# Second attention block in split float32r: 21 weight tiles with low parts by GpSimd, and the gate table's zeros issued by GpSimd

## What is computed

```python
mod = silu(c) @ ada_w + ada_b              # six vectors: shift, scale, gate, twice
h = modulate(rmsnorm(x, norm1_g), shift1, scale1)
q, k, v, cb, cc, cu = split(h @ w_in)      # widths 512, 128, 128, 512, 512, 512
q, k = rope(rmsnorm(q per head)), rope(rmsnorm(k per head))
attn = sliding_window_attention(q, k, v, sinks)     # window 128, 8 query heads, 2 key heads
conv = cb * short_conv(cc * cu, conv_w)             # 3 taps
merged = concat(rmsnorm(attn), rmsnorm(conv))
x = x + gate1 * (merged @ w_out)
h2 = modulate(rmsnorm(x, norm2_g), shift2, scale2)
x = x + gate2 * peer(h2, ...)   # 16384 experts, 16 chosen by each of 8 heads
```

## Time and profile before

| What | Value |
|---|---|
| profiled execution, its span | 2427.28 us, 2425.5 us |
| TensorE busy, of the span | 2390.9 us (99%) |
| VectorE, ScalarE, GpSimd busy | 1435.7, 874.2, 1045.5 us |
| mean granted TensorE clock | 0.99 |
| feed-forward of the first block | 518.8 to 881.4 us |
| second block up to the output product | 888 to 1122 us |

### The profile page before, as it was taken

The page is one execution under the profiler, slowest core; times in us unless marked ns, Lnnn a source line. Parts: engine busy times, 40 slices in busy tenths (PEclk is TensorE's granted clock), DMA queues, the critical chain, the costliest instruction groups (busy, mean ns, idle before and its releaser), DMA issues.

```text
span 2425.5 us, 33627 instructions
## 1 busy us (share of the span) xinstructions
PE 2390.9 (99%) x11435; PEld 1464.0 (60%) x11435; DVE 1435.7 (59%) x2831; ACT 874.2 (36%) x1385; POOL 1045.5 (43%) x739
## 2 busy tenths in 40 slices
PE   8999899999999999999999999999999999999999
PEld 6888677658888875445454444444444466666665
DVE  4412455456867556544949894222222399999988
ACT  3222223232232242223135655544544433333332
POOL 0001111010000020000888888888888175578666
PEclk9999889999999999999999999999999999999999
DMA  7240100265656312942436666666666799999997
GB/s 207 70 72 1 53 10 10 70 178 156 191 176 205 87 53 70 345 174 87 87 48 153 154 148 153 155 147 154 155 147 156 257 401 375 370 361 375 374 361 287
DMA packets 437701, 426.49 MB, mean 176 GB/s; under 512 B 104809, under 2 KB 359913, under 8 KB 437489
## 3 DMA queue, kind: packets, MB, share of 16 engines
q1 hardware_dynamic: 353456, 332.85, 43.0%
q0 software_dynamic: 84160, 92.58, 15.5%
HBM read 364.28 MB, written 61.05 MB: 175 GB/s over the span
## 4 chain that ended last, share of the span: by engine, by line
PE 96%; DVE 2%; ACT 1%; SPq 0%; issue 0%; DMA 0%; POOL 0%; DVEq 0%; ACTq 0%; POOLq 0%
PE psum L1474 9%; PE psum L1475 9%; PE psum L1476 9%; PE psum L1499 7%; PE psum L1497 7%; PE psum L1498 7%; PE psum L1249 6%; PE psum L889 6%; PE psum L1206 5%; PE psum L1208 5%; PE psum L1207 5%; PE psum L1455 4%; PE psum L1106 1%; PE psum L1083 1%; PE psum L1062 1%; PE psum L1122 1%
## 5 line engine op out<-in xcount | busy, mean ns | idle before, releaser
L786 POOL DMA_INDIRECT dense_gates<-arena x384 | 607.2, 1581 | 151.6 <-issue 116.7
L1474 PE MATMUL psum<-arena 128*128 128x512 bf16 x1024 | 389.4, 380 | 0.0
L1476 PE MATMUL psum<-arena 128*128 128x512 bf16 x1024 | 387.1, 378 | 0.0
L1475 PE MATMUL psum<-arena 128*128 128x512 bf16 x1024 | 386.6, 378 | 0.0
L2545 DVE TENSOR_TENSOR arena<-arena,psum 128x1024 bf16<-128x1024 f32 x124 | 151.5, 1221 | 352.2 <-ACT psum L1855 351.7
L1498 PE MATMUL psum<-arena,low 128*128 128x384 bf16 x1024 | 333.8, 326 | 0.0
L1499 PE MATMUL psum<-arena,low 128*128 128x384 bf16 x1024 | 333.8, 326 | 0.0
L1497 PE MATMUL psum<-arena,low 128*128 128x384 bf16 x1024 | 333.8, 326 | 0.0
L1871 ACT ACTIVATE low<-low 128x1024 bf16<-128x1024 f32 x128 | 135.3, 1057 | 296.3 <-PE psum L1499 282.6
L814 POOL DMA_INDIRECT arena<-gelu_spill,arena x128 | 178.3, 1393 | 87.5 <-DMA gelu_spill<-cst 43.3
L806 POOL DMA_INDIRECT arena<-in_v,arena x128 | 166.3, 1300 | 103.0 <-DVE arena L2592 77.5
(11 more groups left out here) (377 smaller groups left out, 3937.0 us busy)
## 6 DMA issues: line engine op xcount, KB each, us to landing
arena<-in_uT SPq DMA_DIRECT2D x128, 512.0 KB, 4.6
low<-in_v SPq DMA_DIRECT2D x128, 512.0 KB, 5.3
gelu_spill<-cst SPq DMA_DIRECT2D x128, 256.0 KB, 3.4
arena<-in_ada_w POOLq DMA_DIRECT2D x12, 2048.0 KB, 9.3
dense_gates<-arena SPq DMA_DIRECT2D x4, 6144.0 KB, 40.1
arena<-gelu_spill SPq DMA_DIRECT2D x128, 192.0 KB, 5.2
arena<-dense_gates SPq DMA_DIRECT2D x128, 192.0 KB, 6.7
low<-in_w_in SPq DMA_DIRECT2D x20, 1024.0 KB, 7.4
```

Source lines behind the costliest of these rows:

```text
L786: pool.indirect_dma_start(gate_cells, bass.IndirectOffsetOnAxis(ap=cell_of[:, n:n + 1], axis=0), gate_of[:, n:n + 1], None, compute_op=ALU ...
L1474: mm(psum[:, bank, :], hi[:, c, :], h2hi[:, c, :], start=c == 0, stop=False)
L1475: mm(psum[:, bank, :], hi[:, c, :], h2lo[:, c, :], start=False, stop=False)
L1476: last = mm(psum[:, bank, :], lo[:, c, :], h2hi[:, c, :], start=False, stop=c == DC - 1)
```

## The change

Twenty-one tiles of the second block take the split form: query tiles 2 and 3, the key tile, all tiles of `cc`, `cu` and `cb`, and output tiles 2 to 7 (`ITEMS_2`, in TensorE's order). High parts are written by ScalarE (`split_high_2`; in the loop at the steps in `SPLIT_AT`), low parts by GpSimd (`split_low_2`), into the three buffers of the feed-forward. The activations get high parts from ScalarE (`bhi`) and low parts from VectorE (`blo`), once for the normed input and once for the merged one. The last norm leaves VectorE and becomes two multiplications over all of `xT2` on GpSimd, after its ninth low part. The weight fills wait for GpSimd's low parts (`fw_lo`), and the next fill is issued earlier than before in places. The zeros of `dense` are written by 16 transfers on GpSimd's queue, of 8 rows of experts each: two after each of the last four `load_ada`, and eight more after these. The buffers are laid out anew for it (those lines are left out here).

```diff
+        ITEMS_2 = [("q", 2), ("q", 3), ("k", 0)]
+        ITEMS_2 += [(what, j) for j in range(4) for what in ("cc", "cu")] + [("cb", j) for j in range(4)]
+        ITEMS_2 += [("o", f) for f in range(2, DC)]
+        SPLIT_AT = [(6, 7), (8,), (9, 10), (11,), (12, 13), (14,), (15, 16), (17,)]
...
@@ SyncE
+                sp.wait_ge(S["fw_lo"], F_ALL + 2 + k)
                 fill(F_CU2 + k, ...
-                     "p2_ready", 4 if k == 0 else 5 + SC)
-            fill(F_CB2, halves(F_CB2, w2[:, :, c_cb:c_cb + 512]), "p2_ready", 5 + SC + 2)
-            sp.wait_ge(S["pool_step"], 10)
-            for q in range(4):
-                sp.dma_start(io["dense"][q * 32:(q + 1) * 32, :, 0:DEN].rearrange("i j t -> j i t"),
-                             zeros.unsqueeze(1).to_broadcast([P, 32, DEN])).then_inc(S["zeroed"], 16)
+                     "p2_ready", 2 if k == 0 else 5 + SC)
+            fill(F_CB2, halves(F_CB2, w2[:, :, c_cb:c_cb + 512]), "fw_lo", F_ALL + place_2["cc", 2])
...
-                fill(F_OUT2 + k, ..., "p2_ready", 5 + SC + 4 * (k + 1))
+                fill(F_OUT2 + k, ..., "fw_lo", F_ALL + place_2[("cb", 0) if k == 0 else ("o", 2)])
...
@@ GpSimd
+            def clear(q):
+                pool.dma_start(io["dense"][q * 8:(q + 1) * 8, :, 0:DEN].rearrange("i j t -> j i t"),
+                               zeros.unsqueeze(1).to_broadcast([P, 8, DEN])).then_inc(S["zeroed"], 16)
...
                 load_ada(k)
+                if k == 6:
+                    pool.wait_ge(S["tab"], 1)
+                    step(pool.memset(zeros, 0.0))
+                elif k > 7:
+                    pool.wait_ge(S["pool_step"], 10)
+                    clear(2 * k - 16)
+                    clear(2 * k - 15)
+            for q in range(8, 16):
+                clear(q)
...
+            def split_low_2(i):
+                pool.wait_ge(S["fw_hi"], F_ALL + i + 1)
+                pool.tensor_tensor(fwl[i % SPLITS], raw_2(i)[1], fwh[i % SPLITS], ALU.subtract).then_inc(S["fw_lo"], 1)
+
+            for i in range(place_2["o", 5]):
+                split_low_2(i)
+                if i == 8:
+                    pool.wait_ge(S["x2_ready"], 1)
+                    pool.tensor_tensor(xT2, xT2, col_ln[:, 0:DC].unsqueeze(2).to_broadcast([P, DC, SEC]), ALU.mult
+                                       ).then_inc(S["x2_ready"], 1)
+                    pool.wait_ge(S["x2_ready"], 2)
+                    pool.tensor_tensor(xT2, xT2, r2[:, 1, :].unsqueeze(1).to_broadcast([P, DC, SEC]), ALU.mult
+                                       ).then_inc(S["x2_ready"], 1)
+                elif i == 16:
+                    add_square(sqc, 1, "m_sq", 2)
             for c in range(1, DC - 1):
                 add_square([u2[:, i, :] for i in range(DC)], c, "sq_ready", 3 * DC + c + 1)
+                if 2 <= c < 5:
+                    split_low_2(place_2["o", c + 3])
...
@@ TensorE (product becomes product_2 for the 21 tiles)
+            def product_2(bank, i, sig, between=None):
+                pe.wait_ge(S["fw_lo"], F_ALL + i + 1)
+                wh, wl = fwh[i % SPLITS], fwl[i % SPLITS]
                 for c in range(DC):
                     if between and c == 4:
                         between()
+                    mm(psum[:, bank, :], wh[:, c, :], bhi[:, c, :], start=c == 0, stop=False)
+                    mm(psum[:, bank, :], wh[:, c, :], blo[:, c, :], start=False, stop=False)
+                    last = mm(psum[:, bank, :], wl[:, c, :], bhi[:, c, :], start=False, stop=c == DC - 1)
+                last.then_inc(S[sig], 1)
...
@@ ScalarE
+            def split_high_2(i):
+                if i < SPLITS:
+                    act.wait_ge(S["ffn_ps"], F_ALL)
+                else:
+                    sig, count = done_2(i - SPLITS)      # product i - 3 has ended
+                    act.wait_ge(S[sig], count)
+                n, w = raw_2(i)
+                if i == 0 or raw_2(i - 1)[0] != n:
+                    act.wait_ge(*fill_done(n))
+                f_(fwh[i % SPLITS], w, ACT.Copy).then_inc(S["fw_hi"], 1)
+            for c in range(DC):
+                act.wait_ge(S["shifted"], c + 1)
+                f_(bhi[:, c, :], u2[:, c, :], ACT.Copy).then_inc(S["h2_hi"], 1)
+                if c >= DC - SPLITS:
+                    split_high_2(c - (DC - SPLITS))
...
                 ins.then_inc(S["a_tc"], 1)
+                for i in SPLIT_AT[s]:
+                    split_high_2(i)
...
+            for c in (4, 5, 6, 7, 0, 1, 2, 3):
+                act.wait_ge(S["m_done"], (c + 4) % DC + 1)
+                f_(bhi[:, c, :], mix[:, c, :], ACT.Copy).then_inc(S["h2_hi"], 1)
...
@@ VectorE
             modulated(0, col_n1, DC)
+            for c in range(DC):
+                dve.wait_ge(S["h2_hi"], c + 1)
+                dve.tensor_tensor(blo[:, c, :], u2[:, c, :], bhi[:, c, :], ALU.subtract).then_inc(S["h2_split"], 1)
             dve.wait_ge(S["std_ready"], 5)
             settle(dve.reciprocal(r2[:, 1, :], r2[:, 1, :]))
-                if j < 4:
-                    last_norm(2 * j)
-                    last_norm(2 * j + 1)
...
+            dve.wait_ge(S["zeroed"], 256)                # ahead of the attention loop
...
+            for k, c in enumerate((4, 5, 6, 7, 0, 1, 2, 3)):
+                dve.wait_ge(S["h2_hi"], DC + k + 1)
+                dve.tensor_tensor(blo[:, c, :], mix[:, c, :], bhi[:, c, :], ALU.subtract).then_inc(S["h2_split"], 1)
             for f in range(DC):
                 dve.wait_ge(S["out2_done"], f + 1)
+                dve.wait_ge(S["x2_ready"], 3)
```

More of the change, by code:

```diff
@@ L135, in program @@
         with nc.sbuf_tensor("split", [P, SPLIT_FLOATS], F32R) as split:
+            pass
+        with nc.sbuf_tensor("below", [P, BELOW_2], F32), nc.sbuf_tensor("split_2", [P, 2 * DC * SEC], F32R) as split_2:
             pass
@@ L271, in program @@
         keep = top[0]
+        sq2 = carve(2, SEC)
+        tm2 = carve(2, SEC)
+        pT2 = carve(2, PER * P)
+        assert top[0] == CUT + BELOW_2
+        bhi, blo = (split_2[:, k * DC * SEC:(k + 1) * DC * SEC].rearrange("p (c t) -> p c t", c=DC) for k in range(2))
+        top[0] += 2 * DC * SEC
+        mxs, nms, rss, ess = (carve(PER) for _ in range(4))
+        assert top[0] <= ffn_end - 2 * SPLITS * DC * P
+        top[0] = ffn_end
+        cosT, sinT, angT = (carve(SEC) for _ in range(3))
+        assert top[0] <= over_rstd - MOD_W
+        vt2 = angT.rearrange("p (a b) -> p a b", a=SC)
+        ex = carve(PER, 2 * P)
+        mix = carve(DC, SEC)
+        y2 = carve(CW // P, SEC)
+        over_zeros = arena_floats - (DC * SEC + P + SEC + DEN)
+        assert top[0] <= over_zeros
+        top[0] = over_zeros + DEN
         qkr = carve(5, SEC)
-        vt2 = carve(SC, P)
         prod = carve(2, SEC + CK2 - 1)
         cc = carve(2, SEC)
[L276 to L285, removed]
         top[0] = over_rstd + 2 * TP
         kf, posi = carve(SEC), carve(SEC)
+        zeros = kf[:, 0:DEN]
         assert top[0] <= base2
@@ L316, in program @@
         gate_of = carve(SEC)
-        zeros = carve(DEN)
+        assert top[0] == over_zeros, (top[0], over_zeros)
+        top[0] += DEN
         slot_row = carve(P).bitcast(U32)
@@ L393, in raw_done, with raw_2, done_2 @@
             return S[f"landed{r}"], before + 32 * (e // RAWS + 1)
+        F_ALL = len(ITEMS_F)
+        ITEMS_2 = [("q", 2), ("q", 3), ("k", 0)]
+        ITEMS_2 += [(what, j) for j in range(4) for what in ("cc", "cu")] + [("cb", j) for j in range(4)]
+        ITEMS_2 += [("o", f) for f in range(2, DC)]
+        place_2 = {item: i for i, item in enumerate(ITEMS_2)}
+        def raw_2(i):
+            what, j = ITEMS_2[i]
+            n = {"q": F_Q2, "k": F_KV2, "cc": F_CU2 + j // 2, "cu": F_CU2 + j // 2, "cb": F_CB2, "o": F_OUT2 + j // 4}[what]
+            if what in ("cc", "cu"):
+                w = slot[n % 2].rearrange("p (g c n) -> p g c n", g=2, c=DC)[:, what == "cu"]
+                return n, w[:, :, j % 2 * P:(j % 2 + 1) * P]
+            return n, slot_cols(n, 256 if what == "k" else 512)[:, :, j % 4 * P:(j % 4 + 1) * P]
+        def done_2(i):
+            what, j = ITEMS_2[i]
+            return {"q": ("p2_ready", j + 1), "k": ("p2_ready", 5), "cc": ("ffn_ps", F_ALL + j + 1),
+                    "cu": ("p2_ready", 5 + SC + j + 1), "cb": ("p2_ready", 5 + SC + 4 + j + 1), "o": ("out2_done", j + 1)}[what]
         def chunks_of(i):
@@ L1278, in _ @@
             for f in range(2, 5):
-                n, k = (F_Q2, f) if f < 4 else (F_KV2, 0)
-                if k == 0:
-                    pe.wait_ge(*fill_done(n))
+                if f == 2:
+                    pe.wait_ge(S["h2_split"], DC)
                 pe.wait_ge(S["p2_taken"], f - 1)
-                product(f % 2, slot_cols(n, 512 if f < 4 else 256), slice(k * P, (k + 1) * P), u2, "p2_ready")
+                product_2(f % 2, f - 2, "p2_ready")
                 qk_mean(f - 1)
```

55 lines of the change are left out of this document (22 added, 33 removed).

## The result

| | us |
|---|---|
| before, median of 20 runs | 2427.17 (2418.12 to 2428.89) |
| changed, median of 20 runs | 2434.5 (2426.21 to 2438.15) |
| ratio, 95% interval | 1.0027 (1.0017 to 1.0037) |
| profiled execution, its span | 2434.32, 2432.5 |

The changed kernel is slower by 0.27%, where 3.5 us faster was forecast. Its trace is cut at the same landmarks as that of before: the first and last start of one line's instructions, as in the earlier trace rows.

What follows compares the result with a forecast made beforehand. TensorE was taken to bound the kernel, holding 96% of the chain of waits. Terms -2.6 + 1.3 - 7.2 + 3 + 2 = -3.5 on 2427.28 gave 2423.8 us profiled, 2423.2 as median; range 2405 to 2435.

Steps and rivals of the forecast that it cites:

- Feed-forward and DMA: Zeros on GpSimd's queue between the modulation loads of the feed-forward: last load up to 7 us late, priced at +2 us.
- The rival of the slow modulation load: Feed-forward's second part: below about 205 GB/s VectorE's wait for the last modulation load decides; 2430 to 2438 us, chance 0.12.
- a TensorE gap in the feed-forward over 5 us: One of the signs listed beforehand that would show the forecast wrong.
- Stage A: From the first norm to the first scores, 4 tiles: -5.6 us before waits, -2.6 with them.
- Stage B: The eight attention steps, 11 tiles: 17.7 us gained against 19.0 of waits, so +1.3 us.
- the clock: TensorE's granted clock falls to 0.50 after a long wait in the attention loop: +3 us, bounds 0 and 6.
- The exclusion: VectorE operations with two SBUF inputs and GpSimd tensor operations exclude each other; attention steps wait 19.0 us in all.
- Step 2: Attention step with GpSimd's two 4096-column multiplications, 7.4 us each; they hold up VectorE's small operations and TensorE waits 9.1 us.
- steps 1, 3, 5 and 7: Attention steps where GpSimd's subtractions hold up VectorE's small operations: waits of 2.9, 1.8, 2.1 and 3.1 us.
- Stage C: Merge and output, 6 tiles: -8.4 us before waits, -7.2 with them.
- The zeros leave SyncE's queue at no gain: Taking the zeros off SyncE's queue gains nothing, since nothing on the chain of waits waits for them.
- The forecast's rule of two SBUF inputs: VectorE operations with two SBUF inputs and GpSimd tensor operations exclude each other for their whole length.

Runs made afterwards that it cites:

- x2: The kernel before with only the zeros moved, to 16 GpSimd transfers in the feed-forward; 2442.13 us, ratio 1.0066 to before.
- x1: The changed kernel with the zeros again written by four SyncE transfers in the second block, the 21 tiles kept; 2419.2 us, ratio 0.9971 to before.
- x3: The changed kernel with the same 16 clears spread, four behind one modulation load, then one per later feed-forward tile; 2420.87 us, ratio 0.9969 to before.

## Why the prediction was wrong

**The step that failed is "Feed-forward and DMA", a term of +2 that measured +14.1.** It asked who waits for the zeros and who stands behind them in GpSimd's queue, and found the modulation load, 0 to 4 us late, and nobody else: "Clears 6 to 15 (15.7 MB, 70 us at 225) pass by about 865, ahead of VectorE's new wait at the loop". It named the transfers and their 70 us, and didn't ask which other queue uses the same DMA engines in those 70 us. The feed-forward's weight loads do, one pair for every two tiles, and their landing is what TensorE's splits wait for. The rival of the slow modulation load reached the right total (2430 to 2438) by the wrong road: the slowest load landed after 13.6 us, and its sentence "weight loads share the engines" had the sharing the wrong way round. It was set aside with "every load of before lands at 225 GB/s beside them"; 9.3 us, from which that figure comes, is the median, and the slowest of before's twelve took 13.7. The sign of error that the prediction named, "a TensorE gap in the feed-forward over 5 us", is what the trace shows (7.98 the longest).

The waits are not the whole of it: they sum to 10.8. Behind the longest the granted clock is 0.50, and twelve products start 0.43 us apart instead of 0.23, which is 2.5 us of the other 3.3.

**Stage A, forecast -2.6, measured -3.9.** The last two low parts of the activations meet GpSimd as worked out (L2424 twice in 4.49 us), and the second tile starts at 918.6, where the forecast, moved by the 13.2 us of the later feed-forward, gave 919.5.

**Stage B, forecast +1.3 and +3 for the clock, measured +4.0 with both in it.** The exclusion was right, but the sum is right by luck, from terms that were each off. Step 2 waits 9.61 (9.1 forecast); steps 1, 3, 5 and 7 wait 1.77, 0, 1.22 and 1.92 (2.9, 1.8, 2.1 and 3.1): 14.5 in all instead of 19.0. The tiles took back some 3 us of that. The forecast set 7.10, a recorded length, against 5.49, a distance between starts. By distances a tile of the loop took 6.97 us (1018.03 to 1025.00, before) and takes 5.62 (1022.87 to 1028.49, after), so eleven gain 14.9, not 17.7; the forecast's own "29.4 us at most" for all 21 was less than the 31.7 that its three stages add up to. The clock, 8 us at 0.50, cost 4 us, more than the +3. Together -14.9 + 14.5 + 4 is 3.6 of the 4.0. The multiplications took 7.02 and 8.91 (7.4 each), the low part 2.00 (2.2).
The Trainium skill (GPSIMD Engine Reference, 3.1 Elementwise), by whose 4497 ns for 2048 columns I had estimated 9.0 for 4096, fits the second of the two and is too dear for the first.

**Stage C, forecast -7.2, measured -7.9.** Right within a microsecond.

**"The zeros leave SyncE's queue at no gain"** was right: A, B and C of x2, which has only the zeros moved, are those of before to 0.1 us.

In sum the forecast missed the profiled execution by 10.5 us (+7.0 instead of -3.5): 12.1 from the feed-forward's term, -1.3, -0.3 and -0.7 from A, B and C, and +0.7 from parts that the change doesn't touch. The range, 2405 to 2435, held the 2434.5 by half a microsecond, and not for a reason that the prediction gave.

## What to carry to other kernels

A bulk transfer that nobody waits for is not free: list every queue that moves data in its time, and how much lead the loads of the critical stage have; then issue the bulk in pieces paced by that stage's own progress, or behind its last urgent loads (16 paced clears cost nothing here, nor did five in one lot behind those loads; ten at once ahead of them cost 14 us). A GpSimd operation beside a chain of small VectorE operations holds the chain up until it ends, and TensorE pays what the chain's slack doesn't cover (9.61 us in step 2, of 15.9 us of multiplications); cutting it into pieces doesn't help if they run back to back; give the work to the engine of the chain, behind the operation that releases TensorE. Price a long TensorE wait with the slower clock after it (4 us behind those 9.61).

## What the runs showed of the hardware beside this

- With ten clears queued on GpSimd, SyncE took 10.74 to 14.31 us for the issue alone of one 512 KB load; GpSimd issued its ten clears in 8.96 us, 0.9 each.
- Not every operation of VectorE stands still beside GpSimd: in step 2 an addition that reads PSUM (L2492) and a reduction with one input (L2494, above) took their usual 1.22 us inside the two multiplications; the next one, with two inputs in SBUF, waited. The forecast's rule of two SBUF inputs is too narrow, though: in step 1 an operation with one tensor input (L2496, a multiplication of four columns by a constant) took 1.93 us instead of 0.17 and ended at 969.21, where GpSimd's two low parts end at 969.19.
- The two GpSimd multiplications of one size differ: 7.02 us where one factor is a column repeated along the row, 8.91 where it is a row repeated over the chunks. In pieces of 512 columns they take 1.04 and 1.29.
- Executions differ by more than the change: the feed-forward began at 509.4 us in x1's trace and at 526.9 in x3's, though the two kernels do the same ahead of it. Lengths of one stage (361.9, 361.9, 362.0) told the kernels apart where whole executions of one kernel scatter by 12 us (x1: 2409.99 to 2421.88).
